# Mixture-of-experts decoder block: the w_down loads of passes 1 to 14 are issued from ACT's DMA queue, the w_up loads from SP's

## The reference

```python
def clamped_swiglu(hu):
    glu, lin = hu[..., ::2], hu[..., 1::2]
    glu = jnp.minimum(glu, SWIGLU_LIMIT)
    lin = jnp.clip(lin, -SWIGLU_LIMIT, SWIGLU_LIMIT)
    return glu * jax.nn.sigmoid(SWIGLU_ALPHA * glu) * (lin + 1.0)

def moe(h, w_router, b_router, w_up, b_up, w_down, b_down):
    ...
    gates = jnp.einsum('tk,tke->te', top_w, jax.nn.one_hot(top_idx, N_EXPERTS, dtype=jnp.float32))
    for e in range(N_EXPERTS):
        act = clamped_swiglu(t @ w_up[e] + b_up[e])
        out = out + gates[:, e:e + 1] * (act @ w_down[e] + b_down[e]).astype(jnp.float32)
```

## Time and profile before

| | |
|---|---|
| median of three runs | 1110.59 us (1110.28 to 1111.09) |
| the profiled execution | 1109.44 us |
| its span | 1107.5 us |
| TensorE matmuls | 1029.6 us busy, 93% of the span |
| weight loads of TensorE | 499.7 us, 45% |
| DVE, ACT, GpSimd | 252.0, 104.6, 21.5 us |
| moved by DMA | 430.00 MB, of it 427.05 MB over SP's queue |
| granted TensorE clock, mean | 0.982 |

### The profile page before, as it was taken

How to read it: one execution, slowest core, us unless ns; L and a number is a source line. 1 busy time by engine, 2 the same in 40 slices (tenths; PEclk the granted TensorE clock), 3 DMA queues, 4 the chain that set the end, 5 groups by cost and what they waited for, 6 DMA issues and landing times.

```text
span 1107.5 us, 11484 instructions
## 1 busy us (share of the span) xinstructions
PE 1029.6 (93%) x4968; PEld 499.7 (45%) x4968; DVE 252.0 (23%) x578; ACT 104.6 (9%) x238; POOL 21.5 (2%) x28
## 2 busy tenths in 40 slices
PE   7999999999999998989898989898989989898996
PEld 6888887433343434333333424243434333333332
DVE  2231124412121212121212112031212121212111
ACT  2131012100000000000000000010100000000002
POOL 1100002000000000000000000000000000000010
PEclk9999999999999999999999999999999999999998
DMA  9803993899999999999999999999999999999995
GB/s 326 308 1 107 423 417 141 368 429 428 427 428 427 427 428 428 428 427 428 425 430 427 426 427 430 428 426 428 427 427 430 428 427 427 429 427 429 426 418 194
DMA packets 46207, 430.00 MB, mean 388 GB/s; under 512 B 7843, under 2 KB 9548, under 8 KB 21068
## 3 DMA queue, kind: packets, MB, share of 16 engines
q1 hardware_dynamic: 40672, 427.05, 91.9%
q10 hardware_dynamic: 5180, 1.14, 0.5%
q0 software_dynamic: 304, 1.06, 0.3%
HBM read 428.17 MB, written 1.06 MB: 388 GB/s over the span
## 4 chain that ended last, share of the span: by engine, by line
PE 57%; DMA 41%; DVE 1%; issue 0%; SPq 0%; ACT 0%; ACTq 0%; POOL 0%; POOLq 0%; DVEq 0%
DMA ring<-in_w_down 29%; PE bank L913 19%; PE bank L982 15%; DMA ring<-in_w_up 11%; PE bank L685 9%; PE bank L1010 4%; PE bank L789 3%; PE bank L868 2%; PE bank L696 1%; PE bank L897 1%; DMA small<-in_norm_g 1%; PE bank L906 1%; PE bank L817 0%; PE bank L705 0%; PE bank L824 0%
## 5 line engine op out<-in xcount | busy, mean ns | idle before, releaser
L913 PE MATMUL bank<-ring,z_buf 128*64 128x512 f32 x2048 | 467.0, 611 | 45.9 <-issue 25.3
L913 PEld LDWEIGHTS bank<-ring,z_buf 128*64 128x64 f32 x2048 | 156.5, 140 | 340.6 <-issue 340.4
L982 PE MATMUL bank<-ring,h_buf 128*64 128x512 f32 x1024 | 226.9, 595 | 7.4 <-DMA ring<-in_w_down 6.6
L982 PEld LDWEIGHTS bank<-ring,h_buf 128*64 128x64 f32 x1024 | 78.7, 137 | 133.1 <-issue 130.6
L1309 DVE TENSOR_SCALAR swi<-bank 128x256 f32<-128x256 f32 x62 | 26.3, 425 | 309.7 <-PE bank L913 304.8
L685 PE MATMUL bank<-h_buf,ring 128*128 128x256 f32 x336 | 75.7, 380 | 0.0
L685 PEld LDWEIGHTS bank<-h_buf,ring 128*128 128x128 f32 x336 | 63.5, 190 | 8.8 <-issue 0.2
L868 PE MATMUL bank<-u_buf,m_buf 128*128 128x128 f32 x512 | 62.6, 275 | 0.0
L614 ACT ACTIVATE swi<-swi 128x256 f32<-128x256 f32 x62 | 25.9, 417 | 384.4 <-DVE swi L1309 384.4
L868 PEld LDWEIGHTS bank<-u_buf,m_buf 128*128 128x128 f32 x512 | 60.0, 193 | 0.8 <-issue 0.8
L1010 PE MATMUL bank<-y,u_buf 128*128 128x512 f32 (+1 forms) x132 | 59.5, 593 | 0.5 <-DVE y L1325 0.5
(11 more groups left out here) (187 smaller groups left out, 398.8 us busy)
## 6 DMA issues: line engine op xcount, KB each, us to landing
ring<-in_w_up SPq DMA_DIRECT2D x126, 2048.0 KB, 36.8
ring<-in_w_down SPq DMA_DIRECT2D x58, 2048.0 KB, 36.8
ring<-in_w_in SPq DMA_DIRECT2D x6, 2048.0 KB, 19.7
ring<-in_w_down SPq DMA_DIRECT2D x10, 1024.0 KB, 27.5
ring<-in_w_out SPq DMA_DIRECT2D x2, 2048.0 KB, 16.5
ring<-in_w_up SPq DMA_DIRECT2D x4, 1024.0 KB, 35.4
ring<-in_w_pool_proj SPq DMA_DIRECT2D x1, 2048.0 KB, 25.8
ring<-in_w_attn_proj SPq DMA_DIRECT2D x1, 2048.0 KB, 27.2
```

What stands on the lines that cost most here:

```text
L913: ins = nc.tensor.matmul(up_banks[j][e * SLOTS:(e + 1) * SLOTS, :], xgT[:, k, e * SLOTS:(e + 1) * SLOTS], w[e].rearrange("p (k n) -> p k n ...
L982: ins = nc.tensor.matmul(down_banks[n][e * SLOTS:(e + 1) * SLOTS, :], hidT[:, k, e * SLOTS:(e + 1) * SLOTS], w[e], start=(k == 0), stop=(k ...
```

## The change

In passes 1 to 14 (`from_act`) the four w_down loads leave SP's loop, and ACT issues them (`load_down`): loads 8 and 9 of pass g + 1 at the end of ACT's part of pass g, behind the copy of line 618 and a wait for `down_done`; loads 10 and 11 at the start of ACT's part of pass g + 1, ahead of `copy_spreadT`, behind a wait for `up_done` (k0). Slots, sizes, sources and semaphores stay the same. Passes 0 and 15 are as before.

```diff
+def from_act(g, load):
+
+    return FIRST < g < LAST and load >= UP_LOADS
...
-                    if (g, load) in IN_PARTS:
+                    if (g, load) in IN_PARTS or from_act(g, load):
                         continue
...
+            def load_down(g, m):
+
+                if m == 0:
+                    act.wait_ge(down_done, MH * g)
+                else:
+                    act.wait_ge(up_done, (KK - 1) * g + 1)
+                for e in range(2):
+                    slot = slot_of(g * LOADS + UP_LOADS + 2 * m + e)
+                    src = w_down_d[2 * g + e:2 * g + e + 1, m * CH:(m + 1) * CH, :].rearrange("e (p k) n -> p (e k n)", p=P)
+                    act.dma_start(ring[:, slot, :], src).then_inc(full[slot], LANDED)
+
-            def act_pass(g, first=False, last=False):
+            def act_pass(g, first=False, last=False, loads_down=False, next_loads_down=False):
+                if loads_down:
+                    load_down(g, 1)
                 copy_spreadT(g)
...
                 nc.scalar.copy(y[:, 0:CH], down_banks[0][:, :]).then_inc(y0_copied, 1)
+                if next_loads_down:
+                    load_down(g + 1, 0)
 
             for g in range(PASSES):
-                act_pass(g, first=(g == FIRST), last=(g == LAST))
+                act_pass(g, first=(g == FIRST), last=(g == LAST), loads_down=from_act(g, UP_LOADS),
+                         next_loads_down=from_act(g + 1, UP_LOADS))
```

## The result

The changed kernel takes **1121.31 us** (1119.97 to 1121.56, four runs) against 1110.83 of the kernel before in the same runs: ratio 1.0098, interval 1.0086 to 1.0111, 10.5 us slower. The forecast was 1120.0, within 1108 to 1134.

The account below looks back on a forecast made before the run. The prediction took DMA to pace passes 5 to 14 and TensorE to set the end from pass 15. 1109.44 + 0 (issues) + 0 (bytes) + 9.3 (landing order) gave 1118.8 us profiled, 1120.0 as median, range 1108 to 1134.

Parts of the forecast that it names:

- The bound: Whole kernel: DMA paces passes 5 to 14 at 4.93 us a load; TensorE sets the end from pass 15.
- 30.2 us of "issue": TensorE's waits in passes 5 to 14, read as standing at k2 and being the DMA wait under another name.
- The terms at 0: Bytes moved by DMA and the 56 issues shifted from SP to ACT: both claimed to cost 0.
- The order: Landing order: w_down skips SP's backlog, queues share one for one, w_up lands at half speed; +9.3 us at the end.
- The walk: Pass-by-pass reckoning of w_up landings and k3 stops; pass 15 starts at 1056.1 against 1045.65, 10.4 us late.
- Every even pass not at all: From pass 5 on, every odd pass stops 13 us at k3, every even pass has no stop.
- The sum: Whole kernel: 1109.44 + 0 (issues) + 0 (bytes) + 9.3 = 1118.8 us profiled; median 1.15 above, so 1120.0.
- the phase of the alternation: Last k3 stop falls in pass 13; in pass 12 the loss would be +2.3 us, in pass 14 +17.
- No change: Rival 1, whole kernel: bytes set the pace and nothing else shows; 1110 to 1113 us; chance 0.15.
- Faster by a better filled DMA: Rival 2, DMA engines: two queues fill them better; 1108 us at a rate 1.4% higher; chance 0.13.
- The Trainium skill's rule: DMA queues: several issuing engines share the same 16 engines and save only sequencer time; by it alone 1110.6 us.
- Worse than the walk: Rival 3, DMA queues: shares not one for one, or rate lost to switching; 1128 us at 1% lower; chance 0.14.

Follow-up runs that it names:

- passes 1 to 12 alone: The changed kernel with ACT issuing the w_down loads in passes 1 to 12 only, 13 and 14 back on SP: 1110.01 us, ratio 0.9997.
- pass 14 alone: The changed kernel with ACT issuing w_down loads in pass 14 only, 4 loads in place of 56: 1127.02 us, ratio 1.0145.
- the run to 13: The changed kernel with ACT issuing w_down loads in passes 1 to 13, pass 14 back on SP: 1121.47 us, ratio 1.0099.
- rows cut in two: The changed kernel with each 16 KB row of ACT's loads written as two halves of 8 KB within one DMA: 1121.19 us, ratio 1.0095.
- the cut packets: The changed kernel with each of ACT's loads issued as two DMAs of 1 MB with rows of 8 KB: 1142.89 us, ratio 1.0291.
- the second pair alone: The changed kernel with ACT issuing only loads 10 and 11 of passes 1 to 14, the rest on SP: 1119.66 us, ratio 1.0087.
- the late issue: The changed kernel with ACT issuing loads 8 and 9 only behind k0, together with the second pair: 1136.06 us, ratio 1.0216.
- the first pair: The changed kernel with ACT issuing only loads 8 and 9 of passes 1 to 14, 10 and 11 on SP: 1117.68 us, ratio 1.0066.
- first probe: The changed kernel with all weights on SP; ACT keeps its waits and four DMAs a pass, each 128 rows of 4 bytes: 1114.77 us, ratio 1.0033.
- second probe: The first probe with each of ACT's DMAs bringing one row of 4 bytes in place of 128: 1110.57 us, ratio 1.0002.

## Why the prediction was right, point by point

**The bound.** DMA sets the pace of passes 5 to 14, TensorE the end from pass 15 on. Shown: stops of 9 to 12.5 us up to pass 11 cost nothing (passes 1 to 12 alone), while four loads in pass 14 make pass 15 start 19.5 us late and cost 16.3 us (pass 14 alone). One reading was rough: not all of the 30.2 us of "issue" stands at k2; 6.8 stands at the transpose ahead of k1 (line 876 in the earlier trace rows). Nothing in the sum hangs on it.

**The terms at 0.** Bytes: 427 to 428 GB/s with both queues full. Issues: 1110.57 us with ACT's waits and issues alone. Both are shown.

**The order.** One for one in packets: 361 and 363, then 397 and 395 with packets of unlike size. The walk against the trace, stops at k3 in us:

| pass | 2 | 3 | 4 | 5 | 7 | 8 | 9 | 11 | 12 | 13 | 14 | start of 15 |
|---|---|---|---|---|---|---|---|---|---|---|---|---|
| walk | 1.3 | 13.4 | 0 | 12.8 | 13.4 | 0 | 12.8 | 13.4 | 0 | 12.8 | 0 | 1056.1 |
| measured | 1.19 | 12.20 | 0 | 12.52 | 7.07 | 2.23 | 12.54 | 8.46 | 2.35 | 12.54 | 0 | 1058.37 |

Passes 6 and 10 are 0 in both. "Every even pass not at all" was too neat: where the stop of an odd pass comes out 5 to 6 us shorter (7, 11), the next one has 2 us of it. The mean is the same, as it must be when the DMA sets it.

At the start of pass 15 the walk is 2.3 us short. Most of that is made in pass 13, the last with a stop. It starts 0.8 us behind the walk (938.79 against 938.0), pass 14 already 2.3 (1006.57 against 1004.3). There TensorE waits 0.74 us at k2 too, where the walk has nothing, and the block behind the stop takes 9.35 us, where the walk had 8.7. The mixer is no explanation: pass 1 starts 1.3 us later here than before (242.57 against 241.24), but with ACT in passes 1 to 13 it starts at 241.25, and pass 15 still at 1058.79.

**The sum** said +9.3. Between the profiled executions, which is what it was worked out for, 11.7 were measured, between the medians 10.5. The forecast added 1.15 us because the profiled execution of before lies that far below its median; with the change the two are only 0.1 apart (1121.18 and 1121.31). So 1.0 of the nearness of 1120.0 to 1121.31 is chance. And the number hangs on the phase of the alternation: by the prediction's own bounds a last stop one pass earlier or later makes it +2.3 or +17. The phase held in the two other executions that go to pass 13 or 14 (the run to 13 and the one with rows cut in two): their last long stop is in pass 13 too. The landing time of w_down, 21.9 us, fell in the 20 to 25 that was named.

**The rivals.** No change: it needs the last stop in pass 12 or earlier, and the run with ACT in passes 1 to 12 is just that case, 1110.01. Faster by a better filled DMA: the split of every pair over both queues gives 0.9998, so nothing was left to fill. The Trainium skill's rule (page "DMA: Bandwidth & Descriptors", section "Issuing engines are not separate DMA queues") holds for the rate; what that section leaves out, who lands first, made the 10.5 us. Worse than the walk: not this change, but the cut packets (+32.5) show the way; the prediction's price for ACT's smaller share was "tens of us". The +16.3 of pass 14 alone lies near the prediction's +17 for a last stop in pass 14, but in another kernel, with more loads overtaken, and doesn't bear that number out.

**Where later expectations missed:** the size was too low for the second pair alone (by 2.4 us over the top of the range), the late issue (by some 5) and the cut packets (by 8.5), and barely for the first pair (by 0.4). The late issue and the cut packets were priced with a DMA that keeps its full rate; the pairs with more waiting to give up in pass 15 than the 1.09 us of the earlier trace rows, and with a start of pass 15 that is 8 to 9 us late, where 9.5 and 11.4 were measured.

## What to carry to other kernels

Where transfers are the bound and one queue already holds them in order of use, as here, a second queue added no bandwidth; it handed out shares, one packet for one, and let late-wanted data land ahead of early-wanted data. Before moving a load to another queue, ask what stands ahead of it in the old one, and who waits for that. If two queues are needed, split each pair of loads over both instead of giving each queue its own kind; and look at the last stages first, since a consumer with slack wins back earlier lateness for nothing.

## What the runs showed of the hardware that was not expected

- The first probe's tiny DMAs cost 4.2 us (1114.77 against 1110.57), though they carry 28 KB. Its queue shows 144 packets for each DMA (5760 for 40 from 454 to 1045 us), the second probe's 2 (80 for 40), so 7952 packets more in the 56 DMAs. With 16 engines that is an estimated 8.5 ns of an engine for each (4.2 x 16 / 7952).
- Writing a contiguous row of 16 KB as two of 8 KB changes nothing in the packets (13244 both times); two DMAs for each load do (21308).
- In a stop of 18 us TensorE stood at half of its clock, 1.2 GHz, and it was back at 2.4 GHz from 600 us on (the stretches shown with the cut packets). The two stretches before (busy of TensorE first, then after the five engines the granted clock), in the run with cut packets:

```profile
580.00:590.00 10.00, 1.14 (x4) 0.58 (x6) 0.00 (x0) 0.00 (x0) 0.00 (x0) 0.50 1.01 427
590.00:600.00 10.00, 10.00 (x40) 3.19 (x38) 0.76 (x2) 0.58 (x1) 0.00 (x0) 0.82 0.99 410
```

  In the changed kernel the block behind a stop of 12 us takes 8.7 to 10.0 us in place of 7.1 (granted clock 0.78 from 380 to 390 us, in pass 3). Up to pass 11 this costs nothing, since the DMA sets the pace there. In pass 13, behind the last stop, it counts: 9.35 us in place of 7.09 is 2.3 us of the lateness at the start of pass 15.
